# Other start addresses for the 256-column operands of a float32r matmul kernel

## The reference

```python
def _ffn_half(h, g, shift, scale, gate, w_in, w_out):
    a, b = jnp.split(_modnorm(h, g, shift, scale) @ w_in, 2, axis=-1)
    return h + 0.5 * gate * ((jax.nn.silu(a) * b) @ w_out)

def _swiglu(h, wg, wu, wd):
    return (jax.nn.silu(h @ wg) * (h @ wu)) @ wd

def second_block(x, ...):
    h = x
    for l in range(DEPTH):
        f = _swiglu(_rmsnorm_2(h, ff1_norm_pre[l]), ff1_w_gate[l], ff1_w_up[l], ff1_w_down[l])
        h = h + 0.5 * _rmsnorm_2(f, ff1_norm_post[l])
        m = _hybrid_mixer(_rmsnorm_2(h, mix_norm_pre[l]), w_in[l], ...)
        h = h + _rmsnorm_2(m, mix_norm_post[l])
        f = _swiglu(_rmsnorm_2(h, ff2_norm_pre[l]), ff2_w_gate[l], ff2_w_up[l], ff2_w_down[l])
        h = h + 0.5 * _rmsnorm_2(f, ff2_norm_post[l])
    return h
```

## Time and profile before

| | us |
|---|---|
| median of 3 runs | 2794.99 |
| lowest and highest run | 2784.18, 2798.64 |
| span of the profiled execution | 2785.2 |
| TensorE busy in it | 2699.6 |
| weight loads | 2437.4 |
| VectorE busy | 1698.2 |
| ScalarE busy | 1128.0 |

### The profile page before, as it was taken

How to read it: one execution, slowest core, us unless ns; L and a number is a source line. 1 busy time by engine, 2 the same in 40 slices (tenths; PEclk the granted TensorE clock), 3 DMA queues, 4 the chain that set the end, 5 groups by cost and what they waited for, 6 DMA issues and landing times. The chain is left out here.

```text
span 2785.2 us, 43819 instructions
## 1 busy us (share of the span) xinstructions
PE 2699.6 (97%) x18136; PEld 2437.4 (88%) x18136; DVE 1698.2 (61%) x2099; ACT 1128.0 (40%) x1409; POOL 0.9 (0%) x13
## 2 busy tenths in 40 slices
PE   7999999999999999999999999999999999998998
PEld 5878878878888888888998999999979999997998
DVE  6774655777325753444456655765877666587764
ACT  5222223522224222225244544544544444454543
POOL 0000000000000000000000000000000000000000
PEclk9999999999999999999999999999999999999999
DMA  8663631456323654544222666566526656652564
GB/s 271 209 183 113 188 118 46 136 182 191 95 93 101 200 184 132 171 145 126 87 85 82 186 193 189 166 209 192 160 61 192 193 165 192 194 173 69 164 191 131
DMA packets 377431, 428.76 MB, mean 154 GB/s; under 512 B 14016, under 2 KB 359488, under 8 KB 377152
## 3 DMA queue, kind: packets, MB, share of 16 engines
q1 hardware_dynamic: 376416, 424.79, 49.8%
q10 hardware_dynamic: 864, 1.80, 0.2%
HBM read 425.49 MB, written 1.05 MB: 153 GB/s over the span
## 5 line engine op out<-in xcount | busy, mean ns | idle before, releaser
L724 DVE TENSOR_TENSOR w_lo<-raw,w_hi 128x1024 fp32r<-128x1024 f32 (+1 forms) x672 | 799.1, 1198 | 809.9 <-ACT w_hi L715 803.2
L715 ACT ACTIVATE w_hi<-raw 128x1024 fp32r<-128x1024 f32 (+1 forms) x672 | 690.9, 1036 | 1022.5 <-PE ps L1090 902.6
L1088 PE MATMUL ps<-u_hi,w_hi 128*128 128x256 f32 (+1 forms) x3168 | 1004.4, 317 | 10.7 <-DVE tmp L1040 4.4
L1090 PE MATMUL ps<-u_hi,w_lo 128*128 128x256 f32 (+1 forms) x3168 | 998.0, 315 | 0.0
L1089 PE MATMUL ps<-u_lo,w_hi 128*128 128x256 f32 (+1 forms) x3168 | 997.9, 315 | 0.0
L1088 PEld LDWEIGHTS ps<-u_hi,w_hi 128*128 128x128 f32 x3168 | 597.2, 189 | 64.2 <-issue 16.9
L1090 PEld LDWEIGHTS ps<-u_hi,w_lo 128*128 128x128 f32 x3168 | 595.5, 188 | 41.3
L1089 PEld LDWEIGHTS ps<-u_lo,w_hi 128*128 128x128 f32 x3168 | 595.7, 188 | 41.0
L1088 PE MATMUL ps<-g_hi,w_hi 128*128 128x256 f32 (+1 forms) x1408 | 449.9, 320 | 0.0
L1090 PE MATMUL ps<-g_hi,w_lo 128*128 128x256 f32 (+1 forms) x1408 | 449.2, 319 | 0.0
L1089 PE MATMUL ps<-g_lo,w_hi 128*128 128x256 f32 (+1 forms) x1408 | 449.2, 319 | 0.0
(11 more groups left out here) (271 smaller groups left out, 2265.4 us busy)
## 6 DMA issues: line engine op xcount, KB each, us to landing
raw<-in_ffn_w_in SPq DMA_DIRECT2D x176, 512.0 KB, 4.4
raw<-in_w_mod SPq DMA_DIRECT2D x128, 512.0 KB, 4.4
raw<-in_ff_w_gate SPq DMA_DIRECT2D x88, 512.0 KB, 4.4
raw<-in_ff_w_up SPq DMA_DIRECT2D x88, 512.0 KB, 4.3
raw<-in_ffn_w_out SPq DMA_DIRECT2D x64, 512.0 KB, 3.4
raw<-in_ff_w_down SPq DMA_DIRECT2D x64, 512.0 KB, 3.6
raw<-in_ret_w_in SPq DMA_DIRECT2D x48, 512.0 KB, 3.5
raw<-in_w_in SPq DMA_DIRECT2D x36, 512.0 KB, 3.8
```

What stands on the lines that cost most here:

```text
L715: act.activation(w_hi[:, slot, unit_at(g, cols)], raw[:, raw_slot, 0:cols], ACT.Copy).then_inc(hi_ready, 1)
L724: dve.tensor_tensor(w_lo[:, slot, at], raw[:, raw_slot, 0:cols], w_hi[:, slot, at].bitcast(f32), ALU.subtract).then_inc(lo_ready, 1)
L1088: pe.matmul(out, w_hi[:, slot, cols], hi, start=first, stop=False, **check)
L1090: return pe.matmul(out, w_lo[:, slot, cols], hi, start=False, stop=last, **check)
```

## The change

Four places change. `SHIFT` goes from 48 to 16 elements, from 192 to 64 bytes. A new constant `BOTH_SHIFT` of 48 elements moves the weights of q and gate within their slot, where they are split and where they are read. An unused piece of 48 elements (192 bytes) is put ahead of `g2_hi`, which moves `g2_hi` and `g2_lo` to 155136 and 177664.

```diff
-SHIFT, ROOM = 48, 64
+SHIFT, BOTH_SHIFT, ROOM = 16, 48, 64
...
-        tables, poolw, g2_hi, g2_lo = overlay(tab_spec + [
-            ("g2_hi", [P, FT, SEQ], f32r), ("g2_lo", [P, FT, SEQ], f32r)])
+        tables, poolw, _, g2_hi, g2_lo = overlay(tab_spec + [
+            ("g2_room", [P, 48], f32), ("g2_hi", [P, FT, SEQ], f32r), ("g2_lo", [P, FT, SEQ], f32r)])
...
         def unit_at(g, cols):
 
-            at = SHIFT if g.mode == "tokens" and cols <= KT_MAX * UCOLS else 0
+            at = SHIFT if g.mode == "tokens" and cols <= KT_MAX * UCOLS else BOTH_SHIFT if g.more.get("both") else 0
             return slice(at, at + cols)
...
         def pe_block(pe, g, it, u, pair, b, k0, k, first, last):
 
-            slot, cols = u % RING, slice(k * UCOLS + b * P, k * UCOLS + b * P + P)
+            at = unit_at(g, 0).start + k * UCOLS + b * P
+            slot, cols = u % RING, slice(at, at + P)
```

## The result

The changed kernel takes 2810.86 us (median, 2809.11 to 2813.88), the kernel before beside it 2790.78 us (2784.18 to 2798.64). The ratio is 1.0069, 95% interval 1.0045 to 1.0093: slower by 0.7%. The forecast was 2772 us and faster; the time lies at the top of the stated range, where the fourth rival stands.

A forecast was written before the change was run, and what follows sets the result against it. TensorE, busy 97% of the span, was taken to bound the kernel through its matmul pitch. 2785.2 - 10.0 - 2.4 - 3.9 = 2768.9 us, plus 3 us for stretches staying slow: 2772, range 2763 to 2812.

The forecast's parts named there:

- fourth rival: Slower: the load sets the pitch, every triple at 64 loses two slots; 2805 us, 2822 with (b) at +13.7; 25%.
- (a): u, first-block g and v, 7,728 matmuls from 192 to 64: always fast saves 10.0 us, always slow costs 24.0.
- (b): g2, 2,112 matmuls from 192 to 128: -2.4 us if fast, +13.7 us if as in pool_v's 264-column half.
- (c): q and gate, 192 + 384 matmuls from distance 0 to 64: saves 3.9 us at 113.3 ns, 1.3 at 117.8.
- rival 3: 64 is fast and 128 is not: 2785 us, 12%.
- Rival 2: 64 has two pitches as 192 does, with another share of slow stretches; (c) gains 1 to 4: 2781 to 2797, 18%.

The follow-up runs named there:

- the scans: The kernel before with a tail of short unwaited matmul streams at chosen start addresses behind its last GEMM, run once each; pitches read from traces, 113.3 to 130.0 ns.
- at_112: The changed kernel with all the moved 256-column GEMMs set to distance 112 instead of 64 or 128: 2775.27 us against 2785.57 for the kernel before, ratio 0.9961.
- mix_112: at_112 with q's and gate's weights at 64 bytes, distance 192, instead of 144: 2775.01 us against 2794.61 for the kernel before, ratio 0.9934.
- u_only: The kernel before with only SHIFT (tokens and v's weights) moved to 64 bytes: 2805.97 us against 2787.46, ratio 1.0056.
- scan_columns: The kernel before with a tail of 24 triples each at 256 to 320 columns and distances 0, 64, 128, 192; at 264 columns 120.0 to 121.0 ns.

## Why the prediction was wrong
**What bounds the kernel: right.** Only addresses changed, and the time followed the matmul pitch: +28.9 us in the GEMMs, +24.7 in the span.

**The two pitches and their lock: right, and not followed far enough.** The prediction saw that a pitch holds until a wait; in the first matmuls behind one it can still turn fast, as the scans show. The 45 ups at 192 and 64 show that the same code settles at either. The mix of slow GEMMs in the one profile before was a draw, and the kernel before spreads over 22 to 25 us in its groups of 13 to 19 times, where at_112 and mix_112 spread over 7 to 8 in ten.

**The step that failed: "I take the fast value for 64 and for 128."** Its reason was a picture, a stream that starts ahead of the load and pulls away. No row showed it, nor that anything happens in steps of 64 bytes; the scans contradict it: 64 ended at 117.8 ns in all six scan streams and in 8 of 10 ups, 128 118.5 to 120.0 in every stretch. The fast pitch at 64 exists (two ups of u_only), so what the change lost in (a) is the odds of getting it, against 28 of 35 ups at 192; what it lost in (b) is a slower pitch, 118.7 instead of 113.3.

**The sizes in the fourth rival.** (a) at 64 was put at +24.0 and measured +21.1. (c) was -1.3 and is -1.1. (b) was +13.7 and is +8.9. Half of that difference is an error of the sum: 2,112 x 6.5 ns counts from all four downs fast, but one was slow in the profile and already held 2.4 us, so rival 4's 2822 and rival 3's 2785 are each 2.4 us too high. The other half is 118.7 ns instead of the 119.8 taken over from 264-column rows, which scan_columns shows to be mostly a matter of width. With the 4 us that came back elsewhere, the span is 2809.9.

**The other rivals.** Rival 3 had the sign of (b) right but not of (a). Rival 2, that 64 has two pitches as 192 has, describes the mechanism best; its share of slow stretches came out at most of them, which is the price of rival 4. Rival 4's time is the nearest, and it is the only reason why the range reached 2811; but its mechanism, two slots lost in every triple at 64, fails on the two fast ups of u_only. The spread did shrink, from 14 us to 5 over four times each, but not for the reason given: the changed kernel is steadily slow. The forecast's floor, 2768.9 us with every stretch fast, was about right: at 112 the spans are 2775.6 and 2772.4, with q and gate still slow. It took other addresses than the prediction's to come near it.

**The rule against the change.** By the Trainium skill, "TensorE: Matmul & The Clock Gate", Part 2, step 1, a load of the next weights takes no read bandwidth from the running matmul. By that alone the distance would not matter. The measurements decide otherwise for these operands: between 113.3 and 130.0 ns by start address alone, at the same clock. Whether read bandwidth is what is lost, no run shows.

## What to carry to other kernels
Where each matmul of 256 to 320 columns comes with its own weight load, as here, treat start addresses as a parameter, and judge one by whether slow streams become fast at it each time, not by whether a fast stretch was seen there. A scan of short unwaited streams behind the kernel's end finds candidates in one run, where reasoning from the neighbouring rows failed; one stream for each is not enough, as 192 showed, slow in one tail and fast in two others. Keeping the distance the same from one GEMM to the next that follows it without a wait kept the pitch in all 33 downs here.

## What the runs showed that was not expected
The pitch at 112 bytes repairs itself: from 114 to 121 ns to 113.3 within some ten matmuls in the kernel, with nothing waited for. At 192 this happened in some streams only. 4 bytes further or less, at 108 and 116, it is 120.0 and 121.7, and at 104 it is 130.0. With the weights at 16 or 48 bytes and the tile 112 further on it is lost (120.0), at 32, 64 and 128 it isn't. At 320 columns 5 ns are lost at any distance, and at 512 none. What in the chip makes these patterns was not found: the numbers tell where the fast pitch is, not why.
